# Moving side work between weight halves on VectorE and ScalarE: decay gates, solve copies, one norm and four output gates

## The reference, cut to what matters

```python
def first_block(...):                       # all in float32
    proj = rmsnorm(x, mix_norm) @ w_in      # splits into sq, sk, sv, gq, gk, gv, gz, gb, ga
    sb_out = stick_breaking_attention(sq, sk, sv)          # 8 heads of 128
    gdn_out = gated_deltanet(gq, gk, gv, gz, gb, ga, ...)  # 8 heads of 128
    x = x + concatenate([sb_out, gdn_out]) @ w_out
    x = x + memory_cross_attention(rmsnorm(x), rmsnorm(mem), ...)
    x = x + conv_ffn(rmsnorm(x), w_up, conv_w, conv_b, w_down)
    return rmsnorm(x, final_norm)

def gated_deltanet(q, k, v, z, b_logit, a_logit, ...):
    q, k, v = split(silu(causal_dwconv(concat(q, k, v), conv_w)))
    q, k = l2norm(q) * 128 ** -0.5, l2norm(k)
    beta = sigmoid(b_logit)                                    # the decay gates
    g = -exp(a_log) * softplus(a_logit + dt_bias)
    o = gated_delta_rule(q, k, v, beta, g)   # chunks of 64, a triangular solve in each
    return rmsnorm(o, norm_g) * silu(z)                        # the output gate

def second_block(x, ...):                   # layer 0: fox_attention, layer 1: swa_attention
    p = rmsnorm(x) @ w_in                   # q, k, v, gate (and a forget gate in layer 0)
    y = attention(q, k, v, ...) * silu(gate)
    x = x + y @ w_out
```

## Time and profile before

| | value |
|---|---|
| time, median of 3 runs | 2123.79 us (2123.69 to 2123.81) |
| time of the profiled execution | 2122.97 us |
| its span, first to last instruction | 2121.2 us |
| busy: PE / PEld / DVE / ACT | 99% / 87% / 76% / 63% of the span |
| granted TensorE clock, mean | 1.0 |
| chain that ended last | PE 91%, DVE 6%, ACT 2%, issue 1% |

### The profile page before, as it was taken

How to read it: one execution, slowest core, us unless ns; L and a number is a source line. 1 busy time by engine, 2 the same in 40 slices (tenths; PEclk the granted TensorE clock), 3 DMA queues, 4 the chain that set the end, 5 groups by cost and what they waited for, 6 DMA issues and landing times.

```text
span 2121.2 us, 34696 instructions
## 1 busy us (share of the span) xinstructions
PE 2106.8 (99%) x13490; PEld 1840.3 (87%) x13490; DVE 1616.2 (76%) x2956; ACT 1326.5 (63%) x2610; POOL 14.5 (1%) x28
## 2 busy tenths in 40 slices
PE   9999999999999999999999999999999999999998
PEld 8888888888898888888888888888888888988887
DVE  7898666787788888656888867777686777688874
ACT  7866446775676666544666666555556655567764
POOL 0000000000000000000000000000000000000000
PEclk9999999999999999999999999999999999999999
DMA  7544434565455555656555655555554555554464
GB/s 281 177 155 143 152 110 149 200 236 189 160 191 195 191 194 192 198 191 196 191 197 190 198 189 197 196 184 191 187 188 169 169 199 192 191 166 159 150 209 139
DMA packets 107811, 389.86 MB, mean 184 GB/s; under 512 B 12368, under 2 KB 12624, under 8 KB 106880
## 3 DMA queue, kind: packets, MB, share of 16 engines
q1 hardware_dynamic: 105264, 377.34, 53.7%
q0 software_dynamic: 2096, 10.00, 1.3%
q10 hardware_dynamic: 288, 0.32, 0.0%
HBM read 384.36 MB, written 2.13 MB: 182 GB/s over the span
## 4 chain that ended last, share of the span: by engine, by line
PE 91%; DVE 6%; ACT 2%; issue 1%; DMA 0%; SPq 0%; DVEq 0%; ACTq 0%
PE main L604 85%; PE two L604 5%; DVE W L1111 2%; PE two L607 1%; DVE gt L1111 0%; DVE PPw L1111 0%; ACT L1798 0%; DVE AQ L1111 0%; ACT W L1799 0%; DMA RAW<-ws 0%; ACT PPw L1799 0%; DVE GQ L1117 0%; DVE PB L1111 0%; ACT NT L1799 0%; DVE GK L1117 0%
## 5 line engine op out<-in xcount | busy, mean ns | idle before, releaser
L1799 ACT ACTIVATE W<-RAW 128x512 fp32r<-128x512 f32 x1416 | 877.3, 627 | 603.3 <-PE main L604 597.8
L604 PE MATMUL main<-A,W 128*128 128x256 f32 (+2 forms) x7200 | 1248.5, 333 | 1.7 <-DVE W L1111 1.7
L1111 DVE TENSOR_TENSOR W<-RAW,W 128x512 fp32r<-128x512 f32 x1416 | 955.9, 685 | 348.4 <-ACT W L1799 339.7
L604 PEld LDWEIGHTS main<-A,W 128*128 128x128 f32 (+1 forms) x7200 | 1087.9, 188 | 153.6 <-issue 6.8
L604 PE MATMUL main<-H,W 128*128 128x512 f32 (+1 forms) x1408 | 239.7, 333 | 0.0
L604 PEld LDWEIGHTS main<-H,W 128*128 128x128 f32 x1408 | 212.1, 188 | 27.4
L604 PE MATMUL main<-B,W 128*128 128x512 f32 (+1 forms) x1216 | 197.9, 324 | 0.3 <-DVE B L1111 0.3
L604 PEld LDWEIGHTS main<-B,W 128*128 128x128 f32 x1216 | 177.2, 188 | 20.5 <-issue 0.5
L604 PE MATMUL main<-W,A 128*128 128x512 f32 (+1 forms) x672 | 150.2, 378 | 0.0
L604 PEld LDWEIGHTS main<-W,A 128*128 128x128 f32 x672 | 117.9, 188 | 22.2 <-issue 0.5
L604 PE MATMUL main<-W,B 128*128 128x512 f32 x384 | 88.4, 391 | 0.0
(11 more groups left out here) (327 smaller groups left out, 1392.1 us busy)
## 6 DMA issues: line engine op xcount, KB each, us to landing
RAW<-ws SPq DMA_DIRECT2D x707, 512.0 KB, 3.4
CB<-cscr POOLq DMA_DIRECT2D x4, 1024.0 KB, 4.9
XT<-xT POOLq DMA_DIRECT2D x4, 512.0 KB, 5.9
MS<-memT POOLq DMA_DIRECT2D x4, 512.0 KB, 8.1
xs<-xT SPq DMA_DIRECT2D x7, 256.0 KB, 7.7
out<-YT SPq DMA_DIRECT2D x7, 256.0 KB, 2.5
CST<-cst SPq DMA_DIRECT2D x1, 1272.0 KB, 7.9
G<-g POOLq DMA_DIRECT2D x1, 1024.0 KB, 5.8
```

The source lines that it names most:

```text
L604: return e.matmul(o, l, r, start=start, stop=True, skip_group_check=True)
L1111: return e.tensor_tensor(o, a, b, op)
L1799: return e.activation(o, i, f, bias=bias, scale=scale, accum_out=accum)
```

## The change

The instructions are the same, and only their places in the queues differ; the queues of SP and GpSimd are the same row for row. The change has these parts.

- On VectorE and ScalarE `ba()` stands ahead of the `conv` parts in the list, so in ticks where both are live its rows come first. TensorE's list is not changed.
- On VectorE the copy t3 of each octet level stands ahead of the mask t2.
- The norm of q, second group (`T_L2["q", 1]`), begins one half later, on all engines.
- DeltaNet output gate 1 (`gz(1)`) begins two halves later on VectorE and ScalarE.
- Fox output gates 0 to 2 begin one half later (`T_FGATE`), on ScalarE and VectorE, and on VectorE their first product waits one more tick, so that it stands two halves later there.

```diff
@@ tick tables
-T_L2 = {("q", 0): 29, ("k", 0): 45, ("q", 1): 79, ("k", 1): 95}
+T_L2 = {("q", 0): 29, ("k", 0): 45, ("q", 1): 80, ("k", 1): 95}
...
-T_GZ = [ENDS[f"gz{n // 2}", n % 2] + 3 for n in range(4)]
+T_GZ = [ENDS[f"gz{n // 2}", n % 2] + (5 if n == 1 else 3) for n in range(4)]
...
-T_FGATE = [END[f"ft{g}"] + (2 if g == 3 else 1) for g in range(4)]
+T_FGATE = [END[f"ft{g}"] + 2 for g in range(4)]
@@ octet(g) on VectorE
                     w.wait_ge(qd_pe, pe + 7 + 2 * lev)
+                    w.wait_ge(qd_ac, ac + 4 + lev)
+                    e.tensor_copy(halfs(fl(t3)), two[:, :, 256:512]).then_inc(qd_ve, 1)
                     if lev < 5:
                         tt(t2, t1, bm(K[f"lm{lev + 1}"], 8), ALU.mult).then_inc(qd_mu, 1)
-
-                    w.wait_ge(qd_ac, ac + 4 + lev)
-                    e.tensor_copy(halfs(fl(t3)), two[:, :, 256:512]).then_inc(qd_ve, 1)
@@ gate(g, late) on VectorE
-                yield
+                yield from ticks(1 if late or g == 3 else 2)
                 w.wait_ge(gt_silu, (4 if late else 0) + g + 1)
@@ lists of side parts on VectorE and on ScalarE
-            parts += [(T_CONV[x], conv(*x)) for x in CONVS]
+            parts += [(T_BA, ba())] + [(T_CONV[x], conv(*x)) for x in CONVS]
             parts += [(T_L2[x], l2norm(2 * i, *x)) for i, x in enumerate(L2S)]
-            parts += [(T_BA, ba())] + [(T_OCTET[g], octet(g)) for g in range(2)]
+            parts += [(T_OCTET[g], octet(g)) for g in range(2)]
```

## The result

The changed kernel takes 2129.59 us (median of 8 runs, 2128.43 to 2130.25), where the kernel before takes 2123.74 (8 runs, 2122.86 to 2123.90). The ratio is 1.0028, with a 95% interval of 1.0019 to 1.0036: 5.85 us slower. The forecast was 2128.9, with a range of 2123.6 to 2131.2. The profiled execution of the changed kernel took 2129.6 us, its span 2127.8.

The account below looks back on a forecast made before the run. The prediction took TensorE to bound the kernel, so other engines' order counts only where TensorE waits. Its sum was 2123.79 - 0.5 + 0.3 + 5.3 = 2128.9 us, with a range of 2123.6 to 2131.2.

Parts of the forecast that it names:

- The term that decides: Fox output gates 0 to 2: a closed VectorE-ScalarE loop of 2.04 us per half, about +5.3 us (+1.2 to +6.5).
- both bills: Fox gates: gate 0's delay of 2.9 us and gate 1's +2.45 us, together +5.3 at the weighing.
- Decay gates, octet and norm: Decay gates, octet 0 and norm: gates and norm sum to 0, the copy gives -0.5 us (-1.5 to +0.5).
- Output gate 1: DeltaNet output gate 1: lane 0's wait goes, lane 1 waits 1.3 us; about +0.3 us (-1.1 to +0.8).
- Only gate 1 is paid: Rival, fox gates: slack in ScalarE's exps absorbs gate 0's 2.9 us; about 2126.1 us, chance 0.14.
- The waits go as meant: Rival: loop period under 1.38 us, all five TensorE waits go, 4.4 us; 2119.4 us, chance 0.08.
- the waits only change place: Rival: lane 0 for lane 1, load for load, loops give back the 1.19; about 2123.8 us, chance 0.11.
- The faster case: The rival in which all five TensorE waits go, 4.4 us; 2119.4 us, chance 0.08.
- A table switch costs more than its row: Rival: load ahead of the `gt` exps costs a further 1.38 us of drain; about 2130.3 us, chance 0.07.

Follow-up runs that it names:

- The two kernels on distance and place: Changed kernel, fox gates one half later on both engines: 2121.15 us; kernel before, only VectorE's part of fox gates 0 to 2 one half later: 2130.01 us.

## Why the prediction was right, point by point

**The term that decides: right, in mechanism and size.** The stations of the walk through the fox gates can be found in the trace. The changed kernel's trace runs 0.50 us ahead there; with that added back, forecast and measured are: period 2.04 and 2.03; silu of gate 0 at 1637.45 and 1637.65; `FQ<-main` at 1648.8 and 1648.9; TensorE's wait 2.15 and 2.10; further waits 0.5 to 0.7 together and 0.24 + 0.46; the old wait of 1.19 gone; two loop waits of 0.7 each and two of 0.58 and 0.67; weighing 5.3 later and 5.5. Gate 2 costs nothing, as said. The two kernels on distance and place show that it is the loop, and the single gates that both bills are paid.

**Decay gates, octet and norm: -0.5 forecast, -0.8 in the trace.** The copy was right: -0.5 forecast, -0.65 run alone. I was wrong that the other levels show no wait (0.35 and 0.24 above), but with VectorE full the swap is worth one place on it, however many levels have it. For gates and norm together I had 0, and -0.1 is left for them, but that is luck, since two errors cancel. Run alone, the gates' move is not the +0.2 of my sum without the norm, but +0.6; and the norm's later place, for which I had -0.2, has some -0.7 by difference. Behind the moved load I lost 0.7 at `two<-GK` and 0.4 at the transposes; the starts of the halves show 0.4 in small steps from 93 to 107 us, which the walk doesn't have, then 0.5 and 0.4. The exps end at 112.30 in the new trace, which starts 0.94 late, just where the walk had them (111.36).

**Output gate 1: +0.3 forecast, +0.3 in the trace and alone.** Lane 0's wait went, and lane 1's is 1.37 where I had 1.3.

**The rivals.** "Only gate 1 is paid" falls by the kernel with gate 0 alone (+3.25). "The waits go as meant" and "the waits only change place" fall by the period: it would have had to be under 1.38 us. The faster case's mechanism does hold in the fox gates where both engines are moved by the same: there the 1.19 goes, and the whole kernel gains 2.2 us, half of the 4.4 of that rival. "A table switch costs more than its row": the moved load takes 1.28 us from 109.92, and the exps start at 111.22, 0.02 behind it. The drain that the Trainium skill adds (ScalarE: Activation LUTs, What ACT_TABLE_LOAD costs) is in neither trace, and the 2130.3 that it would have given lies above all eight runs.

**What I had wrong: the clock.** I wrote that nothing hangs on it, because the clock was full before. But I forecast a wait of 2.4 us on TensorE, longer than the 1.3 us or so that the kernel before ever shows in its loop, and didn't ask what such an idle time does. With the low clock the weighing took 1.5 us more. The forecast's terms, with the 5.5 of the traces for the gates, give 5.0 without it, and 5.85 was measured. Executions with the low clock may be what lies between, but that isn't shown: the runs behind the two medians spread by 1.0 and 1.8 us.

## What to carry to other kernels

Where two engines hand a side result back and forth between items of a stream that goes through both, write down for each hand-over what stands between the waiting and the giving instruction on both queues. A step of the side work must not be placed so that the next item on the second engine waits for an item that stands on the first engine behind the reply to that step; then the loop's period is the sum of all four latencies, here 2.03 us against TensorE's 1.38, and moving VectorE's part one item further than ScalarE's is what closed it. A delay on a full queue is not paid where it arises but at the next place without reserve, here 15 us later; and a change is to be read as its parts, since the best version here kept all of it but one tick on one engine.

## What the runs showed of the hardware

- With TensorE's waits of 2.0 to 2.6 us late in the kernel the granted clock fell to the lower level for some 3.4 us in three of nine cases, and not each time at the same place of the same order. It cost 1.5 us at the weighing and nothing where TensorE had to wait for VectorE behind it. In the one profiled execution with the wait filled by matmuls the weighing had full clock, as it had in two of three with an unfilled wait of 2.6 us there.
- The same weight loads ran at one of two paces in the profiled executions. TensorE's weight loads `main<-B,W` from 574 to 594 us, in the trace of before and then of after:

```profile
L604 PEld LDWEIGHTS main<-B,W 128*128 128x128 f32 x171 | 20.2, 188 | 0.0
```

```profile
L604 PEld LDWEIGHTS main<-B,W 128*128 128x128 f32 x175 | 19.9, 188 | 0.0
```

  That is 0.118 us each against 0.114, 0.9 us over the stretch. It is not the change's: the kernel with all three gates moved has the slow pace here, and those with one gate moved the fast one (0.9 us shorter). What sets it stays open.
- By 11 us the halves start 0.5 to 1.45 us later in the thirteen other traces than in that of before, with the same transfers and the same order at the start. The pace and this are of the size of the spread among the runs of one kernel (1.0 us for the kernel before in its first 8 runs, 2.4 in 27 later ones), so parts of a few tenths could be read only from the starts of the halves in the traces.
